# Moving one token subtract a unit from VectorE to GpSimd in the output projection of a two-layer decoder trunk

## The chip, the cores and the metric

The kernel runs on one core of a Trainium2 chip, as one program. The metric is the time of the whole program in device microseconds, and lower is better. Five engines work side by side and meet through semaphores: TensorE (PE; matrix products), VectorE (DVE), ScalarE (ACT), GpSimd (POOL) and SyncE (SP), which here mostly issues DMAs.

## The reference, cut to what matters

The reference is one inference step of a trunk of two layers (one recurrent, one with sliding-window attention) over 2048 prompt tokens and 8 samples, with D = 1024. Each layer ends alike, and the change concerns that end in the second layer:

```python
z = jnp.concatenate([y * jax.nn.silu(g_main), om * jax.nn.silu(g_mem)], axis=-1)   # T x 1536
x = x + z @ w_out[l]                                                               # 1536 x 1024
...
return rmsnorm(x, final_g), ...
```

All is float32. The kernel gets that precision from three passes of a coarser format: each operand is split into a high part (a copy that rounds) and a rest (the value minus the high part), and high times high, high times rest and rest times high are added up.

## The kernel before

Most of the kernel is what comes ahead of this stage: projections, attention and recurrence, up to about 1760 us. The stage of the change is the function `paired`, the last 280 us. It multiplies pairs of token tiles (256 rows) by w_out with Strassen's scheme in Winograd's form: seven products instead of eight. It has 16 units: units 0 to 7 are the eight pairs of token tiles with the first half of the 12 ranks of z, units 8 to 15 the same pairs with the second half, in reverse order. Units 0 and 1 are partly woven into the attention loop ahead; units 1 (its last three products) to 15 follow in `tensor`.

In each unit:

- SyncE loads four blocks of z (`load_z`) into `z_raw`, and the pair's rows of x (`load_x`) after it has stored those of the unit two before. In units 8 to 15 the finished rows are normed and stored as y (`store_y`); the next x goes into their place.
- GpSimd makes four sums of token blocks in place (`sums_tokens`; L2422, L2424, L2426, L2429; 128x384 each): S1, S3, S2, S4. Together with three blocks as loaded (A11, A12, A22) these are the seven token operands, in slots 0 to 6 of `z_raw`: A11, A12, A22, S2, S1, S3, S4.
- ScalarE copies slots 0 to 2 (L2453) and, when GpSimd's fourth sum is done, slots 3 to 6 (L2456) to `z_hi`, the high parts (`tokens_act`).
- VectorE makes the rests `z_lo`, in place over `z_raw`, by three subtracts (`tokens_low`, L2550): slots 0 to 2 (128x1152), slots 3 and 4 (128x768), slots 5 and 6 (128x768).
- TensorE runs seven products (`product`, L2686) in the order P2, P1, P4, P6, P5, P7, P3, each of nine matmuls 128x512 (three thirds k, three passes each). P7 uses slot 5 (S3), P3 slot 6 (S4). P2, P6 and P7 wait for the first, second and third subtract. From the third product on, each waits for the add of two products before.
- VectorE adds each product from its bank to x (`add`, L2566).

The order on each engine is that of its program, and nothing else. VectorE's loop has, for unit u: add P2, P1, P4, P6, then add P5, rest 0 of unit u+1, add P7, rest 1 of unit u+1, add P3, rest 2 of unit u+1. In units 9 and up the norms of the rows finished before stand behind the first or second adds (L2606, L2609). In units 3 to 7 ScalarE also makes the high parts of the weights for units 8 and up, and VectorE their rests (L2543); unit 8 has what is left. One weight block, P3, has its rests made by GpSimd: three subtracts of 128x512 (L2437) between the sums of unit 9 and those of unit 10, and P3 of unit 8 waits for them, a third at a time (`wlop`).

ScalarE's program around there is: keys' DMAs, high parts of P7's weights, first copy of unit 9, high parts of P3's weights, a table load with a square root (L2514), second copy of unit 9 (L2456). Around units 9 to 13 the attention of the 8 samples is woven in (functions named `sm`): TensorE turns sample rows (L1526), GpSimd clears two tiles behind that (L1511, L1512), VectorE works on small tiles (L1653 to L1664), and TensorE takes scores (L1545).

Of the kernel before, what the change touches and what calls it, by code (L numbers as in the profile page):

```python
# [5 lines left out]
F32 = mybir.dt.float32  # L6
F32R = mybir.dt.float32r
ALU = mybir.AluOpType
# [2212 lines left out]
def paired(nc, m, A, outs, it, sm, prior, sums):  # L2221
# [6 lines left out]
    whi, wlo, zhi, zlo, mmd, xn, ss, yn = (signals[n] for n in "whi wlo zhi zlo mmd xn ss yn".split())  # L2228
    sums_z, wlop = prior["tr"], prior["used"]
# [3 lines left out]
    W0, Z0, MM0, XN0, SS0, YN0 = NI, TT, 2 * TP, 2 * TP, 2 * TP, TP  # L2233
    SZ0, WP0 = TP, 4
    LD0, WL0, ONE0 = 16 * (TT // 2), 32, 16

    UNITS, NPROD, KQ = 16, 7, 3
# [5 lines left out]
    P2, P1, P4, P6, P5, P7, P3 = range(NPROD)  # L2243
# [10 lines left out]
    z_raw, z_lo = ([m.at(P + f"z{n}{p}", [128, NPROD, KQ, 128], z_at[p], dt) for p in range(2)] for n, dt in (("raw", F32), ("lo", F32R)))  # L2254
    z_hi = [m.at(P + f"zhi{p}", [128, NPROD, KQ, 128], z_at[p] + NPROD * zq, F32R) for p in range(2)]
# [5 lines left out]
    x_s = m.at(P + "x_s", [128, D], LO + 48 * KB)  # L2261
    w_again = m.at(P + "w_again", [128, NI, D], LO)

    bank = lambda u, i: m.bank[2 * (u % 2) + i % 2]
    sample_bank = m.bank[4]
    phase = lambda u: u // 8
# [145 lines left out]

    def sums_tokens(g, u):
        z, n = z_raw[u % 2], SZ0 + 4 * u
        a21 = z[:, S2, :, :]
        tt = nc.gpsimd.tensor_tensor
        free = lambda i: g.wait_ge(mmd, MM0 + made(u - 2, i)) if u >= 2 else None
        g.wait_ge(*z_loaded(u))  # L2420
        free(P5)
        tt(z[:, S1, :, :], a21, z[:, A22, :, :], ALU.add).then_inc(sums_z, 1)  # L2422
        free(P7)
        tt(z[:, S3, :, :], z[:, A11, :, :], a21, ALU.subtract).then_inc(sums_z, 1)  # L2424
        g.wait_ge(sums_z, n + 2)
        tt(a21, z[:, S1, :, :], z[:, A11, :, :], ALU.subtract).then_inc(sums_z, 1)  # L2426
        free(P3)
        g.wait_ge(sums_z, n + 3)
        tt(z[:, S4, :, :], z[:, A12, :, :], a21, ALU.subtract).then_inc(sums_z, 1)  # L2429

    def pool(g):
        for u in range(UNITS):
            sums_tokens(g, u)
            if u == 9:
                for k in range(KQ):
                    g.wait_ge(whi, W0 + KQ * P3 + k + 2)
                    nc.gpsimd.tensor_tensor(w_lo[1][P3][:, k, :], w_raw[1][P3][:, k, :], w_hi[1][P3][:, k, :].bitcast(F32), ALU.subtract).then_inc(wlop, 1)  # L2437
                sm["pool"](g)
# [10 lines left out]
    def tokens_act(act, u, n):  # L2449
        p = u % 2  # L2450
        if n == 0:
            act.wait_ge(*z_loaded(u))
            nc.scalar.activation(z_hi[p][:, 0:3, :, :], z_raw[p][:, 0:3, :, :], ACT.Copy).then_inc(zhi, 1)  # L2453
        else:
            act.wait_ge(sums_z, SZ0 + 4 * u + 4)
            nc.scalar.activation(z_hi[p][:, 3:7, :, :], z_raw[p][:, 3:7, :, :], ACT.Copy).then_inc(zhi, 1)  # L2456

    def within_act(act, q):
# [81 lines left out]
    def weights_low(v, i, ks=range(KQ)):  # L2540
        for k in ks:
            v.wait_ge(whi, W0 + KQ * i + k + 2)
            nc.vector.tensor_tensor(w_lo[1][i][:, k, :], w_raw[1][i][:, k, :], w_hi[1][i][:, k, :].bitcast(F32), ALU.subtract).then_inc(wlo, 1)  # L2543

    def tokens_low(v, u, n):
        p, e = u % 2, (slice(0, 3), slice(3, 5), slice(5, 7))[n]
        v.wait_ge(zhi, Z0 + 2 * u + min(n, 1) + 1)
        if n == 0:
            v.wait_ge(sums_z, SZ0 + 4 * u + 4)
        nc.vector.tensor_tensor(z_lo[p][:, e, :, :], z_raw[p][:, e, :, :], z_hi[p][:, e, :, :].bitcast(F32), ALU.subtract).then_inc(zlo, 1)  # L2550

    def add(v, u, i):
        extra = 2 if u == UNITS - 1 else 0
        if i == 0:
            v.wait_ge(*loaded_x(u))
            if u in (8, 9):
                v.wait_ge(xn, XN0 + made(u - 1 if u == 8 else u - 3, P3))
        if i in needs:
            v.wait_ge(xn, XN0 + extra + made(u, needs[i]))
        v.wait_ge(mmd, MM0 + (1 if u == UNITS - 1 else 0) + made(u, i))  # L2560
        if i == P7:
            x, y = xt[slot(u)][1][:, :].rearrange("p (n e) -> p n e", n=2), bank(u, i).unsqueeze(1).broadcast_to([128, 2, 512])
        else:
            h, o = part_of[i]
            x, y = xt[slot(u)][h][:, o:o + 512], bank(u, i)
        nc.vector.tensor_tensor(x, x, y, ALU.add).then_inc(xn, 1)  # L2566
# [36 lines left out]
    def norm(v, c, u, h):  # L2603
        n, x = 2 * (u - 8) + 1 - h, xt[slot(u)][h]
        v.wait_ge(ss, SS0 + 2 * n + 2)
        c.link(nc.vector.reciprocal(st[:, 4 + h:5 + h], st[:, 2 + h:3 + h]))  # L2606
        if (u, h) == (8, 0):
            v.wait_ge(fgl, FG0 + 16)
        nc.vector.scalar_tensor_tensor(x[:, :], x[:, :], st[:, 4 + h:5 + h], fg[:, :], ALU.mult, ALU.mult).then_inc(yn, 1)  # L2609

    def add_samples(v, c):
        v.wait_ge(x_ld[2], XS0 + 16)
        v.wait_ge(mmd, MM0 + NPROD * (UNITS - 1) + 1)
        for h in range(2):
            x = x_s[0:NS, 512 * h:512 * h + 512]
            c.link(nc.vector.tensor_tensor(x, x, sample_bank[32 * h + 64:32 * h + 64 + NS, :], ALU.add))
            nc.vector.tensor_tensor(x, x, sample_bank[32 * h:32 * h + NS, :], ALU.add).then_inc(xn, 1)

    def norm_samples(v, c):
        v.wait_ge(ss, SS0 + 2 * (TT - 2) + 2)  # L2620
        c.link(nc.vector.reciprocal(st[0:NS, 8:9], st[0:NS, 7:8]))
        nc.vector.scalar_tensor_tensor(x_s[0:NS, :], x_s[0:NS, :], st[0:NS, 8:9], fg[0:NS, :], ALU.mult, ALU.mult).then_inc(yn, 1)
# [3 lines left out]
    def vector(v, c):  # L2626
        for u in range(1, UNITS):
            for i in range(NPROD):
                if u > 1 or i >= P5:
                    if u == UNITS - 1 and i == 0:  # L2630
                        add_samples(v, c)
                    add(v, u, i)
                if u >= 9 and i in norm_at(u):
                    norm(v, c, u - 1, norm_at(u).index(i))
                if 4 <= u < 8 and i in (0, 2, 3):
                    weights_low(v, u - 4, ((0, 2, 3).index(i),))
                if u == 8 and i < 4:
                    weights_low(v, (P5, P7)[i // 2], ((0, 1), (2,))[i % 2])
                if (u, i) == (9, 2):
                    sm["sum_rows"](v, c)  # L2640
                step = {(9, 6): 0, (10, 5): 1, (11, 3): 2, (12, 1): 3, (13, 0): 4, (13, 4): 5}.get((u, i))
                if step is not None:
                    sm["dve"](v, c, step)
                if (u, i) == (UNITS - 1, P6):
                    norm_samples(v, c)
                if (u, i) == (UNITS - 1, P5):
                    v.wait_ge(ss, SS0 + 2 * (TT - 1) + 1)
                    c.link(nc.vector.tensor_scalar(st[:, 11:12], st[:, 9:10], 1.0 / D, EPS, ALU.mult, ALU.add))
                if u < UNITS - 1 and i >= 4:
                    tokens_low(v, u + 1, i - 4)  # L2650
        last_rows(v, c)

# [12 lines left out]
    def product(pe, u, i):  # L2665
        f, p = phase(u), u % 2
        extra = 2 if u == UNITS - 1 else 0
        if u == 0 and i < 2:
            pe.wait_ge(*after(("b_free", "g_free")[i], NCH * NW + 1))
        if u == 1 and i == 0:  # L2670
            pe.wait_ge(*after("m_ready", it["G"] + it["NQ"]))
        if i in (P2, P6, P7):
            pe.wait_ge(zlo, Z0 + 3 * u + (P2, P6, P7).index(i) + 1)
        if i >= 2:
            pe.wait_ge(xn, XN0 + extra + made(u, i - 2))
        a, al = (z[p][:, of_z[i], :, :] for z in (z_hi, z_lo))
        b, bl = w_hi[f][i], w_lo[f][i]
        for k in range(KQ):
            if u == 0 and k == 0:
                pe.wait_ge(*loaded[0][i])  # L2680
            if (u, i, k) == (0, P3, KQ - 1):
                pe.wait_ge(wlo, W0 + 1)
            if u == 8:
                pe.wait_ge(*((wlop, WP0 + k + 1) if i == P3 else (wlo, W0 + KQ * i + k + 2)))
            for q, (s_, r_) in enumerate(((a, b), (a, bl), (al, b))):
                last = nc.tensor.matmul(bank(u, i), s_[:, k, :], r_[:, k, :], start=(i not in (P6, P7, P3) and k == 0 and q == 0), stop=(k == KQ - 1 and q == 2), skip_group_check=True)  # L2686
        last.then_inc(mmd, 1)
# [399 lines left out]
```

## Time and profile before

| | |
|---|---|
| three runs | 2050.04, 2052.72, 2054.45 us; median 2052.72 |
| profiled execution | 2047.37 us, span 2045.5 us |
| mean granted clock of TensorE | 0.997 |
| busy: TensorE, VectorE, ScalarE, GpSimd | 99%, 64%, 46%, 13% of the span |
| busy in TensorE's L2686 (this stage) | 134.5, 132.5 and 132.2 us in its three passes |

The span is the time from the first to the last instruction of the profiled execution. Busy shares are averages over the whole kernel. The time of an instruction is from its start to its end in the record; where an engine is held while an instruction runs, the record is longer. A matmul of 128x512 is recorded with 0.39 us, but the next starts 0.23 us after it.

### The profile page before, as it was taken

How to read it: one execution, taken by the hardware profiler on the slowest of the kernel's cores; microseconds unless marked ns; L12 is line 12 of the kernel's file. 1: busy time of each engine (PE TensorE's matmuls, PEld its weight loads, DVE VectorE, ACT ScalarE, POOL GpSimd, SP SyncE). 2: the span in 40 equal slices, each digit the busy share in tenths (PEclk: the TensorE clock that was granted, in tenths of full speed). 3: DMA queues.
4: the chain of work that ended last, by engine and by line, in shares of the span. 5: the costliest groups of instructions: out<-in, count | busy, mean ns of one | idle time of the engine just before them, and what ended most of it. 6: DMA issues, size and time to landing. Idle time of an engine off the chain costs nothing.

```text
span 2045.5 us, 34917 instructions
## 1 busy us (share of the span) xinstructions
PE 2020.1 (99%) x14353; PEld 1600.6 (78%) x14353; DVE 1309.9 (64%) x2148; ACT 951.0 (46%) x2061; POOL 274.3 (13%) x249
## 2 busy tenths in 40 slices
PE   9999999999999999999999999999999999999988
PEld 8788887777777777777888888787787778788766
DVE  5845437888888753222634434588888888978766
ACT  6733335778778843212533333444444444422442
POOL 0000002221111100000010000212123330134321
PEclk9999999999999999999999999999999999999999
DMA  9421213442332674354211101222221223777675
GB/s 386 146 65 42 65 39 115 140 137 95 117 107 91 220 257 171 109 191 149 95 58 39 45 20 38 70 86 72 77 78 51 86 71 121 273 248 237 228 276 203
DMA packets 140928, 261.54 MB, mean 128 GB/s; under 512 B 14981, under 2 KB 78501, under 8 KB 136281
## 3 DMA queue, kind: packets, MB, share of 16 engines
q1 hardware_dynamic: 135552, 244.63, 35.0%
q10 hardware_dynamic: 5216, 14.69, 2.0%
q8 instruction: 113, 1.85, 0.4%
q14 instruction: 47, 0.38, 0.1%
HBM read 187.79 MB, written 71.55 MB: 127 GB/s over the span
## 4 chain that ended last, share of the span: by engine, by line
PE 90%; DMA 3%; DVE 3%; ACT 2%; issue 1%; SPq 1%; POOL 0%; ACTq 0%; DVEq 0%; POOLq 0%
PE bank L608 52%; PE bank L2111 12%; PE bank L2686 8%; PE bank L150 2%; PE bank L1174 2%; PE bank L712 2%; PE bank L1160 2%; PE bank L699 2%; DMA in_rows<-in_x_prompt 2%; PE bank L908 1%; PE bank L448 1%; PE bank L628 1%; PE bank L702 1%; DVE wo_lo L1805 0%; DMA op_x<-x_scratch 0%
## 5 line engine op out<-in xcount | busy, mean ns | idle before, releaser
L608 PE MATMUL bank<-x_hi,w_hi 128*128 128x512 f32 x1600 | 636.0, 398 | 0.4 <-DVE w_lo L594 0.4
L608 PE MATMUL bank<-x_hi,w_lo 128*128 128x512 f32 x1600 | 624.1, 390 | 0.0
L608 PE MATMUL bank<-x_lo,w_hi 128*128 128x512 f32 x1600 | 623.2, 389 | 0.0
L608 PEld LDWEIGHTS bank<-x_hi,w_hi 128*128 128x128 f32 x1600 | 300.1, 188 | 96.7 <-issue 35.4
L608 PEld LDWEIGHTS bank<-x_hi,w_lo 128*128 128x128 f32 x1600 | 300.3, 188 | 64.5
L608 PEld LDWEIGHTS bank<-x_lo,w_hi 128*128 128x128 f32 x1600 | 300.5, 188 | 60.8 <-issue 0.7
L2111 PE MATMUL bank<-wo_hi,z_hi 128*128 128x512 f32 x384 | 152.3, 397 | 2.9 <-DVE z_lo L1834 1.2
L2111 PE MATMUL bank<-wo_lo,z_hi 128*128 128x512 f32 x384 | 149.7, 390 | 0.0
L2111 PE MATMUL bank<-wo_hi,z_lo 128*128 128x512 f32 x384 | 149.5, 389 | 0.0
L2686 PE MATMUL bank<-op_whi_p,op_zhi 128*128 128x512 f32 x336 | 134.5, 400 | 10.9 <-DVE op_x L2566 8.4
L758 DVE TENSOR_TENSOR it_P_lo<-bank,it_P_hi 128x512 fp32r<-128x512 f32 x64 | 41.2, 686 | 161.6 <-ACT it_P_hi L753 161.6
L1212 ACT ACTIVATE it_X<-it_X,stat 128x128 f32<-128x128 f32 x256 | 99.2, 389 | 91.4 <-DVE stat L1281 91.4
L653 ACT ACTIVATE it_gh<-bank 128x512 f32<-128x512 f32 x96 | 56.7, 591 | 174.3 <-PE bank L608 172.9
L1338 POOL TENSOR_SCALAR w_raw<-w_raw,prm 128x256 f32<-128x256 f32 x56 | 59.8, 1067 | 545.9 <-PE bank L628 275.1
L2686 PE MATMUL bank<-op_whi_p,op_zlo 128*128 128x512 f32 x336 | 132.5, 394 | 0.0
L2686 PE MATMUL bank<-op_wlo_p,op_zhi 128*128 128x512 f32 x336 | 132.2, 393 | 0.0
L2566 DVE TENSOR_TENSOR op_x<-op_x,bank 128x512 f32<-128x512 f32 (+1 forms) x112 | 85.0, 759 | 61.8 <-PE bank L2686 53.2
L1248 DVE TENSOR_TENSOR it_PTs<-bank,tmask 128x512 f32<-128x512 f32 x128 | 79.5, 684 | 59.3 <-PE bank L150 59.3
L747 ACT ACTIVATE it_Pm<-bank,stat 128x256 f32<-128x256 f32 x128 | 58.9, 472 | 88.2 <-DVE stat L766 88.2
L2111 PEld LDWEIGHTS bank<-wo_hi,z_hi 128*128 128x128 f32 x384 | 72.0, 188 | 24.8 <-issue 3.8
L2686 PEld LDWEIGHTS bank<-op_whi_p,op_zhi 128*128 128x128 f32 x336 | 63.8, 190 | 27.8 <-DVE op_x L2566 10.0
L586 ACT ACTIVATE w_hi<-w_raw,prm 128x256 fp32r<-128x256 f32 x200 | 85.1, 507 | 0.3 <-PE bank L702 0.3
(367 smaller groups left out, 3263.1 us busy)
## 6 DMA issues: line engine op xcount, KB each, us to landing
w_raw<-in_w_items SPq DMA_DIRECT2D x25, 1024.0 KB, 5.1
z_scratch<-it_gz SPq DMA_DIRECT2D x96, 256.0 KB, 2.5
it_cs<-in_rope SPq DMA_DIRECT2D x32, 512.0 KB, 4.1
op_x<-x_scratch SPq DMA_DIRECT2D x28, 512.0 KB, 5.4
z_raw<-z_scratch SPq DMA_DIRECT2D x16, 768.0 KB, 5.0
op_zraw<-z_scratch SPq DMA_DIRECT2D x64, 192.0 KB, 3.4
in_rows<-in_x_prompt SPq DMA_DIRECT2D x4, 2048.0 KB, 27.0
in_x<-in_x_T SPq DMA_DIRECT2D x4, 2048.0 KB, 28.0
```

What stands on the lines that cost most here:

```text
L150: last = nc.tensor.transpose(banks[a][:, 64 * i:64 * i + 64], of(i)[e, :], ident[e, e])
L586: nc.scalar.activation(m.w_hi[w % 2][:, k, :], m.w_raw[w % 2][:, k, :], ACT.Copy, scale=m.prm[:, k, gain(w):gain(w) + 1]).then_inc(S["w_hi ...
L608: last = nc.tensor.matmul(ps, s_, r_, start=(k == 0 and q == 0), stop=(k == KT - 1 and q == 2))
L653: nc.scalar.activation(gh[:, :], PG, ACT.Copy, scale=0.5)
L747: nc.scalar.activation(Pm[:, t, :], (S0, S1)[t // 2][:, (t % 2) * M:(t % 2 + 1) * M], ACT.Exp, bias=negm[:, t:t + 1], scale=MEM_SCALE, acc ...
L758: nc.vector.tensor_tensor(query_half(P_lo, b), (T0, T1)[b].rearrange("p (m t k) -> p m t k", m=2, t=4), query_half(P_hi, b).bitcast(F32), ...
L1212: e = nc.scalar.activation(X[:, j, :], X[:, j, :], ACT.Exp, bias=negm[:, j:j + 1], accum_out=rs[:, j:j + 1])
L1248: r = nc.vector.tensor_tensor(PTs[:, h, a, :].rearrange("p (t b k) -> p t b k", t=4, b=2), by_halves(m.psum, 6, h), m.tmask[:, a, :].rearr ...
L1338: nc.gpsimd.tensor_scalar(raw, raw, m.prm[:, k, gain(w):gain(w) + 1], None, ALU.mult).then_inc(S["zeros"], 1)
L2111: last = nc.tensor.matmul(bank(t, h), s_, r_, start=(first and q == 0), stop=(end and q == 2))
L2566: nc.vector.tensor_tensor(x, x, y, ALU.add).then_inc(xn, 1)
L2686: last = nc.tensor.matmul(bank(u, i), s_[:, k, :], r_[:, k, :], start=(i not in (P6, P7, P3) and k == 0 and q == 0), stop=(k == KQ - 1 and ...
```

## The change

From unit 2 on, the third subtract (slots 5 and 6, the rests of S3 and S4) is GpSimd's and no longer VectorE's. GpSimd does it behind the four sums of the same unit, when ScalarE's second copy of that unit is done, and ahead of whatever its program has next (the sums of the next unit; in unit 9 the three subtracts L2437). It counts on the semaphore of the sums, so their counts move (`sums_at`), as do those of VectorE's rests (`lows_at`). P7 of units 2 and up waits for GpSimd's semaphore. Units 0 and 1 stay as they are. The arithmetic is the same.

```diff
+    sums_at = lambda u: 4 * u if u < 2 else 5 * u - 2
+    lows_at = lambda u: 3 * u if u < 2 else 2 * u + 2
...
+    def tokens_low_pool(g, u):
+        p = u % 2
+        g.wait_ge(zhi, Z0 + 2 * u + 2)
+        nc.gpsimd.tensor_tensor(z_lo[p][:, 5:7, :, :], z_raw[p][:, 5:7, :, :], z_hi[p][:, 5:7, :, :].bitcast(F32), ALU.subtract).then_inc(sums_z, 1)
+
     def sums_tokens(g, u):
-        z, n = z_raw[u % 2], SZ0 + 4 * u
+        z, n = z_raw[u % 2], SZ0 + sums_at(u)
...
     def pool(g):
         for u in range(UNITS):
             sums_tokens(g, u)
+            if u >= 2:
+                tokens_low_pool(g, u)
             if u == 9:
                 for k in range(KQ):
                     g.wait_ge(whi, W0 + KQ * P3 + k + 2)
...
-            act.wait_ge(sums_z, SZ0 + 4 * u + 4)
+            act.wait_ge(sums_z, SZ0 + sums_at(u) + 4)
...
-            v.wait_ge(sums_z, SZ0 + 4 * u + 4)
+            v.wait_ge(sums_z, SZ0 + sums_at(u) + 4)
...
-                if u < UNITS - 1 and i >= 4:
+                if u < UNITS - 1 and 4 <= i < 6:
                     tokens_low(v, u + 1, i - 4)
...
         if i in (P2, P6, P7):
-            pe.wait_ge(zlo, Z0 + 3 * u + (P2, P6, P7).index(i) + 1)
+            if i == P7 and u >= 2:
+                pe.wait_ge(sums_z, SZ0 + sums_at(u) + 5)
+            else:
+                pe.wait_ge(zlo, Z0 + lows_at(u) + (P2, P6, P7).index(i) + 1)
```

## Rows read from the trace of the kernel before

**Rows 1.** The page's first part: busy us, share, instructions.

```profile
PE 2020.1 (99%) x14353; PEld 1600.6 (78%) x14353; DVE 1309.9 (64%) x2148; ACT 951.0 (46%) x2061; POOL 274.3 (13%) x249
```

**Rows 2.** Whom TensorE waited for, 1795 us to the end: total, times, longest.

```profile
PE bank L2686 <- DVE op_x L2566: 7.0, 2, 6.8
PE bank L2686 <- DVE op_zlo L2550: 1.6, 1, 1.6
PE bank L2686 <- issue: 0.6, 1, 0.6
PE bank L1526 <- DVE sm_rows L1520: 0.5, 1, 0.5
```

**Rows 3.** Timeline of TensorE, units 8 to 12: start, duration, [idle before, releaser].

```profile
1898.95 0.47 PE L2686 MATMUL bank<-op_whi_p,op_zhi 128*128 128x512 f32 x1 [0.63 <-issue]
...
1901.10 0.39 PE L2686 MATMUL bank<-op_whi_p,op_zhi 128*128 128x512 f32 x1
...
1903.14 0.40 PE L2686 MATMUL bank<-op_whi_p,op_zhi 128*128 128x512 f32 x1
...
1920.30 0.50 PE L2686 MATMUL bank<-op_whi_p,op_zhi 128*128 128x512 f32 x1 [1.64 <-DVE op_zlo L2550]
...
1924.72 1.92 PE L1545 MATMUL bank<-sm_qs,sm_kw 64*128 64x8 f32 x16
1926.87 0.50 PE L2686 MATMUL bank<-op_whi_p,op_zhi 128*128 128x512 f32 x1 [0.22 <-DVE op_x L2566]
...
1970.97 0.79 PE L2686 MATMUL bank<-op_whi_p,op_zhi 128*128 128x512 f32 x1 [6.80 <-DVE op_x L2566]
...
1974.98 0.54 PE L2686 MATMUL bank<-op_whi_p,op_zhi 128*128 128x512 f32 x1
```

**Rows 4.** Single lines, whole span: durations ns min/median/max, first and last start.

```profile
L2550 DVE TENSOR_TENSOR op_zlo<-op_zraw,op_zhi x48: 945/1194/2147, 1761.0 to 2019.5; 128x768 fp32r<-128x768 f32 x32, 128x1152 fp32r<-128x1152 f32 x16
...
L1341 POOL TENSOR_TENSOR w_lo<-w_raw,w_hi x56: 727/740/1296, 1305.0 to 1685.0; 128x256 fp32r<-128x256 f32 x56
...
L2429 POOL TENSOR_TENSOR op_zraw<-op_zraw x16: 992/1444/2009, 1752.0 to 2007.8; 128x384 f32<-128x384 f32 x16
...
L2437 POOL TENSOR_TENSOR op_wlo_p<-op_wraw_p,op_whi_p x3: 1296/1726/1739, 1894.7 to 1897.7; 128x512 fp32r<-128x512 f32 x3
```

**Rows 5.** Timeline of GpSimd, VectorE and ScalarE in unit 2.

```profile
1816.11 1.01 POOL L2426 TENSOR_TENSOR op_zraw<-op_zraw 128x384 f32<-128x384 f32 x1
1816.21 1.73 DVE L2550 TENSOR_TENSOR op_zlo<-op_zraw,op_zhi 128x768 fp32r<-128x768 f32 x1
...
1817.27 1.55 POOL L2429 TENSOR_TENSOR op_zraw<-op_zraw 128x384 f32<-128x384 f32 x1
...
1818.85 1.50 ACT L2456 ACTIVATE op_zhi<-op_zraw 128x1536 fp32r<-128x1536 f32 x1 [4.80 <-POOL op_zraw L2429]
```

**Rows 6.** Timeline of GpSimd, VectorE and ScalarE in unit 8.

```profile
1894.71 4.69 POOL L2437 TENSOR_TENSOR op_wlo_p<-op_wraw_p,op_whi_p 128x512 fp32r<-128x512 f32 x3 [4.47 <-ACT op_whi_p L2447]
...
1894.82 3.44 DVE L2543 TENSOR_TENSOR op_wlo_p<-op_wraw_p,op_whi_p 128x512 fp32r<-128x512 f32 x2
...
1897.19 1.47 ACT L2456 ACTIVATE op_zhi<-op_zraw 128x1536 fp32r<-128x1536 f32 x1
...
1900.46 1.34 DVE L2550 TENSOR_TENSOR op_zlo<-op_zraw,op_zhi 128x1152 fp32r<-128x1152 f32 x1
```

**Rows 7.** Timeline of ScalarE, VectorE and GpSimd ahead of unit 10.

```profile
1918.10 1.49 ACT L2456 ACTIVATE op_zhi<-op_zraw 128x1536 fp32r<-128x1536 f32 x1 [9.13 <-POOL op_zraw L2429]
...
1918.17 2.08 DVE L2550 TENSOR_TENSOR op_zlo<-op_zraw,op_zhi 128x1152 fp32r<-128x1152 f32 x1 [2.86 <-POOL op_zraw L2429]
...
1918.99 2.13 POOL L2424 TENSOR_TENSOR op_zraw<-op_zraw 128x384 f32<-128x384 f32 x1
```

**Rows 8.** Timeline of ScalarE and VectorE in unit 11.

```profile
1950.63 1.47 ACT L2456 ACTIVATE op_zhi<-op_zraw 128x1536 fp32r<-128x1536 f32 x1
...
1952.57 1.28 DVE L2609 SCALAR_TENSOR_TENSOR op_x<-op_x,stat,op_fg 128x1024 f32<-128x1024 f32 x1
```

**Rows 9.** Windows of 4 us: PE, PEld, DVE, ACT, POOL busy, PEclk, DMA share, GB/s.

```profile
1788.00:1792.00 4.00, 2.59 (x25) 2.08 (x24) 3.96 (x7) 1.17 (x1) 1.34 (x2) 1.00 0.86 314
...
1964.00:1968.00 4.00, 0.17 (x1) 0.00 (x0) 0.00 (x0) 1.16 (x1) 1.70 (x2) 1.00 1.05 395
1968.00:1972.00 4.00, 1.03 (x3) 0.84 (x4) 1.70 (x4) 1.48 (x1) 2.23 (x3) 0.56 1.04 413
```

## What the change should do, predicted before it was measured

> **What bounds the kernel now.** First the page: TensorE is busy for 99% of the span, VectorE for 64%, GpSimd for 13% [rows 1]. So the change can only move the time through TensorE's gaps. The second view is who TensorE waited for, in the stretch in which the changed instruction exists. From 1795 us to the end it waited four kinds of time and 9.7 us in all: 7.0 us for VectorE's adds (6.8 us of it in one piece), 1.6 us for a rest, 0.6 us for "issue" and 0.5 us for the sample rows [rows 2]. The third view, TensorE's timeline, says where: unit 8 before its P7 (0.63 us), before unit 10 (1.64 us) and in unit 10 (0.22 us) [rows 3]. With L1526's these are all of the gaps, and units 2 to 7 have none. A product of nine matmuls takes 2.04 us (P3 of unit 8 starts at 1901.10, the next product at 1903.14 [rows 3]), a unit seven of these, 14.3 us. VectorE keeps up with that nearly everywhere, so its 14 removed instructions are covered by TensorE already.
>
> **What is removed.** In units 2 to 15 VectorE loses one subtract of 128x768 a unit, 14 in all. The shortest of these takes 0.95 us [rows 4], 13.2 us together. On the path that sets the end they are worth only what the gaps give back. Where TensorE has no gap behind VectorE, that is nothing: the matmuls cover it.
>
> **What is added.** GpSimd gets 14 subtracts of 128x768. The trace has none of that size; it has 0.73 us for 256 columns, 0.99 for 384 and 1.30 for 512 at best [rows 4], about 2.2 ns a column on 0.17 us. That makes 1.86 us (bounds: 1.3, the 512 row, and 2.6, two 512s). In a usual unit it is hidden: ScalarE's second copy of unit 4 starts at 1818.85 and takes 1.50 us [rows 5], GpSimd could subtract from 1820.4 to 1822.2, the next four sums are about one unit (14 us) behind the last, and P7 that needs the rest runs a unit later. Unhidden it would cost 1.86 us a unit; I count 0 for all units but 9 and 10.
>
> **The port.** When GpSimd and VectorE both work on tensors in SBUF, one waits until the other's instruction ends. VectorE's subtract begins at 1816.21 and takes 1.73 us instead of 0.95, while GpSimd's runs from 1816.11 to 1817.12; GpSimd's next one begins at 1817.27 and takes 1.55 instead of 0.99, and ends 0.9 us after VectorE's [rows 5]. So they take turns by whole instructions, and a longer GpSimd instruction makes a longer wait. The Trainium skill says the same (SBUF — State Buffer, section "SBUF: two separate sides"): the pair of ports is an exclusive lock and not a split of bandwidth. By that rule the sum below would be as it stands; if the two shared the bandwidth, its first term would be up to 0.9 us smaller.
>
> **Unit 9, where the new wait falls.** In GpSimd's program the new subtract of unit 9 stands ahead of the three subtracts L2437, which make the rests of weight block P3 of unit 8. They have to be there when TensorE comes to P3 (1901.10). Before, they began at 1894.71 and took 4.69 us [rows 6], to 1899.40. Now GpSimd must first wait for ScalarE's second copy of unit 9, which starts only at 1897.19 and takes 1.47 us [rows 6], as weights, a table load and a square root stand ahead of it. Step by step: 1898.7 the wait ends; the new subtract, 1.86 us, to 1900.5; VectorE's subtract of 1152 columns (1.34 us alone [rows 6], about 1.27 behind another) has meanwhile queued and goes next, to 1901.8; first L2437 1.29, to 1903.1; VectorE's subtract of 768 columns, 0.87, and two more L2437, 2.5, to 1906.5. TensorE takes 0.68 us for the last third of P3 and comes to unit 9 at 1907.2 instead of 1903.14: **+4.1 us**. If VectorE never got in between it would be 1898.7 + 1.86 + 3.9 + 0.7 = 1905.2, +2.0, and with 1.3 us for the new subtract +1.5; with 2.6 us for it, and VectorE in between, +4.8. The gap of 0.63 us before P7 goes (the two L2543 that took 3.44 us beside L2437 [rows 6] are alone now), but P3 waits for GpSimd, so this gives nothing. Behind the waiting GpSimd stand only L2437 and, later, the sample memsets and the sums of unit 10, which wait for TensorE's own unit 9 and so move with it.
>
> **Unit 10.** All times here relative to before. GpSimd's sums of unit 11 ran beside VectorE's rests; one of them took 2.13 us [rows 7]. VectorE's first rest took 2.08 us [rows 7] instead of 1.34 and released TensorE at 1920.30. Now GpSimd waits for ScalarE's copy (1918.10, 1.49 us) [rows 7] first: the rest takes 1.34, and TensorE starts 0.73 us earlier. But then the 1.86 us subtract and the four sums run on to 1926 or 1927, beside the small VectorE instructions of the samples, which have to be done before L1545 (1924.72 [rows 3]) and before the add that TensorE waited for at 1926.87. Each can be held up to 1 us. From -0.95 us (0.73 and 0.22 gained, no small one held) to +1.5 us (three held, 0.95 saved). I take **+0.7**, nearer to the upper end, as rows 5 show that any two-input instruction is held.
>
> **Unit 12.** TensorE's 6.8 us are the wait for the tokens' load behind a store of y. The store waits for VectorE's norm at 1952.57, 1.28 us; ScalarE's second copy of unit 12 ends at 1950.63 + 1.47 = 1952.1 [rows 8]. The new subtract starts just there and holds the norm to 1953.96, so it ends 1.4 us later. The DMA engines are full then (share 1.05 with TensorE at 0.17 us of 4 [rows 9]), so what is issued later partly finds the queue emptier: 0 to 1.4, I take **+0.5**. With the engines idle it would be 1.4.
>
> **The clock.** Behind the 6.8 us gap the granted clock fell to 0.56 in that slice; with TensorE busy for 2.59 of 4 us it stayed at 1.00 [rows 9]. In unit 8 it would now do one third of P3, 0.7 us, in the 4.2 us from 1901.1 to 1905.3, which is nearer to the emptier slices of rows 9. The product at the half clock (1.2 GHz) started at 1970.97 and the next at 1974.98, 4.01 us instead of 2.04 [rows 3]. Part of that is hidden by the waits for L2437. Bounds 0 and 2.1; I take **+1.5**.
>
> **The sum.** 4.1 + 0.7 + 0.5 + 1.5 = 6.8 us. The profiled execution took 2047.37 us (span 2045.5 and 1.9 around it) and would take 2054.2; the median of the three runs is 5.35 us higher, which gives 2059.5 us (+0.33%).
>
> **The rivals.** (A) The late rest costs less than 4.1 us: TensorE loses 2.0 to 4 us at P3, the clock holds, unit 10 gives back up to 0.95. The sum is +0.5 to +4, 2053.2 to 2056.8. For it: rows 9 show the clock holding through gaps of 1.4 us, and each term has a low end. Against: L2437's order is fixed, and ScalarE's copy at 1898.7 has no slack. (B) Faster: VectorE sets the pace of a unit, and each subtract taken off it shortens a unit by up to 0.95 us; 14 of them give -13.3, 2039.4 us. It decides where VectorE's work in a unit exceeds TensorE's 14.3 us. Against: TensorE waited for VectorE's adds in two places only [rows 2]; just unit 10 is like this. (C) The change does nothing that is seen: GpSimd's subtract hidden in unit 9 too. That would need ScalarE's copy before 1894.7, and it is 4 us later. Its time would be 2052.7. (D) The 6.8 us gap takes up the delay, if the load that ends it doesn't move with TensorE. The result is 2052.7 to 2054. Against: the norm that starts the store follows a product of unit 11.
>
> **How the numbers follow.** Forecast 0.62, A 0.22, D and C together 0.11, B 0.05. Of no change a measurement of this kernel tells about 0.2%, 4.1 us (2048.6 to 2056.8). The forecast's own range: 5.3 without the fall of the clock, 4.1 if unit 10 and unit 12 cost nothing either, and 4.8 + 1.5 + 1.4 + 2.1 = 9.8 with the high ends, so 2056.8 to 2062.5, and up to 2063.5 should a second place lose its clock. A, C and D lie below 2056.8. The range from 2053.7 to 2063.5 leaves out B, C and the low ends of A and D. Slower 0.62, same 0.33, faster 0.05.
>
> **What would show it.** Right: TensorE's gap ahead of P3 of unit 8 of some 2.5 us and shorter ones between its thirds, released by GpSimd L2437; GpSimd's new line at 1898.7 in its first instruction of that stretch, about 1.86 us each; no gaps in units 2 to 7; the gap at 1920.30 down to 0.9; the norm of unit 10 near 2.7 us long; a granted clock below 1.0 soon after P3. Wrong: the three L2437 done by 1903, a clock of 1.00 through unit 9, or a large gap of unit 12 that is shorter by as much as unit 8 grew.

## The result, and the profile after

| | before | changed |
|---|---|---|
| median of 5 runs each | 2052.72 us | 2060.32 us |
| lowest to highest | 2048.15 to 2056.15 | 2057.48 to 2061.18 |
| profiled execution (span) | 2047.37 (2045.5) | 2061.18 (2059.4) |
| mean granted clock | 0.997 | 0.995 |

The changed kernel is slower: ratio 1.0046, 95% interval 1.0033 to 1.0059. Of 2050 us that is 9.4 us, with 6.8 to 12.1 for the interval; the medians are 7.6 us apart. The forecast was +6.8 us, 2059.5 us, with 2053.7 to 2063.5 for the range. Three executions, one of before and two of an experiment below, ran 22% to 92% longer at a mean clock of 0.505 to 0.750, and no median, interval or ratio here counts them.

In the changed kernel the lines have moved: `product` is L2698 (was L2686), VectorE's `add` L2575 (L2566), its rests L2559 (L2550), ScalarE's second copy L2465 (L2456), the norm L2618 (L2609), GpSimd's rests of weights L2446 (L2437). GpSimd's new subtract is L2420.

The first view is again whom TensorE waited for, from 1795 us on (total, times, longest), to be held against [rows 2]:

```profile
PE bank L2698 <- DVE op_x L2575: 13.5, 7, 6.2
PE bank L1545 <- DVE sm_kw L1658: 1.7, 1, 1.7
PE bank L2698 <- DVE op_zlo L2559: 0.9, 1, 0.9
PE bank L1526 <- DVE sm_rows L1520: 0.6, 1, 0.6
PE bank L2698 <- POOL op_wlo_p L2446: 0.5, 1, 0.5
```

It waited 17.2 us in five kinds, before 9.7 us. VectorE lost 14 instructions and TensorE waits more for VectorE, not less, even without the 2.7 us in the first line that are GpSimd's (see below). Two kinds are new: GpSimd's rests of weights, and VectorE's small instruction L1658. The timeline of TensorE says where; these are all of its gaps from 1795 us to the end except the one of L1526 (0.56 us), and answer to [rows 3]:

```profile
1906.08 0.51 PE L2698 MATMUL bank<-op_whi_p,op_zhi 128*128 128x512 f32 x1 [2.70 <-DVE op_x L2575]
...
1907.98 0.80 PE L2698 MATMUL bank<-op_whi_p,op_zhi 128*128 128x512 f32 x1 [0.55 <-POOL op_wlo_p L2446]
...
1928.33 0.50 PE L2698 MATMUL bank<-op_whi_p,op_zhi 128*128 128x512 f32 x1 [0.90 <-DVE op_zlo L2559]
...
1934.41 1.92 PE L1545 MATMUL bank<-sm_qs,sm_kw 64*128 64x8 f32 x16 [1.68 <-DVE sm_kw L1658]
...
1936.50 0.51 PE L2698 MATMUL bank<-op_whi_p,op_zhi 128*128 128x512 f32 x1 [0.17 <-DVE op_x L2575]
...
1965.50 0.47 PE L2698 MATMUL bank<-op_whi_p,op_zhi 128*128 128x512 f32 x1 [0.32 <-DVE op_x L2575]
...
1968.31 0.50 PE L2698 MATMUL bank<-op_whi_p,op_zhi 128*128 128x512 f32 x1 [0.50 <-DVE op_x L2575]
...
1981.11 0.79 PE L2698 MATMUL bank<-op_whi_p,op_zhi 128*128 128x512 f32 x1 [6.19 <-DVE op_x L2575]
...
2020.55 0.50 PE L2698 MATMUL bank<-op_whi_p,op_zhi 128*128 128x512 f32 x1 [2.17 <-DVE op_x L2575]
...
2024.32 0.47 PE L2698 MATMUL bank<-op_whi_p,op_zhi 128*128 128x512 f32 x1 [1.43 <-DVE op_x L2575]
```

Units 2 to 7 still have no gap. The same places of the program in both profiled executions give the loss as a running difference:

| place | before | changed | difference |
|---|---|---|---|
| last gap of unit 1 (1.41 us in both) | 1789.93 | 1793.09 | 3.2 |
| add behind P2 of unit 9 | 1905.51 | 1914.24 | 8.7 |
| sample rows L1526 | 1912.11 | 1920.84 | 8.7 |
| first product of unit 10 | 1920.30 | 1928.33 | 8.0 |
| L1545 | 1924.72 | 1934.41 | 9.7 |
| product behind the add in unit 10 | 1926.87 | 1936.50 | 9.6 |
| product behind the large gap, unit 12 | 1970.97 | 1981.11 | 10.1 |
| end of span | 2045.5 | 2059.4 | 13.9 |

The first 3.2 us lie ahead of everything that the change touches. There TensorE waited 1.5 us more for the first weights' loads and 1.7 us more for rests of the first layer's output, and the other profiled executions below have this place between 1789.85 and 1791.83. So these are no part of the change, and the change's share of this execution is 10.7 us: 5.6 in units 8 and 9, 0.9 in unit 10, 0.5 to unit 12, 3.8 behind it.

How unit 8 came to it, from the timelines of ScalarE, GpSimd and VectorE of the changed kernel (against [rows 6]):

```profile
1900.19 1.47 ACT L2465 ACTIVATE op_zhi<-op_zraw 128x1536 fp32r<-128x1536 f32 x1
...
1901.74 1.84 POOL L2420 TENSOR_TENSOR op_zlo<-op_zraw,op_zhi 128x768 fp32r<-128x768 f32 x1 [8.50 <-ACT op_zhi L2465]
1903.54 2.39 POOL L2446 TENSOR_TENSOR op_wlo_p<-op_wraw_p,op_whi_p 128x512 fp32r<-128x512 f32 x1
...
1901.97 2.82 DVE L2559 TENSOR_TENSOR op_zlo<-op_zraw,op_zhi 128x1152 fp32r<-128x1152 f32 x1
1904.72 1.21 DVE L2575 TENSOR_TENSOR op_x<-op_x,bank 128x1024 f32<-128x1024 f32 x1
1905.85 0.95 DVE L2559 TENSOR_TENSOR op_zlo<-op_zraw,op_zhi 128x768 fp32r<-128x768 f32 x1
```

GpSimd is idle for 8.50 us and starts when ScalarE's copy ends at 1901.7. VectorE's subtract comes 0.2 us later and takes 2.82 us instead of 1.34: held to 1903.54, then alone to 1904.8. Only then does L2446 run, in 2.39 us from its start in the record, to 1905.93, and TensorE's P3 starts at 1906.08. The page's cause for that gap, "DVE op_x", is the semaphore that came last by its estimate. The program makes P3 wait for the add of P5 and for L2446; that add ran from 1901.37 us and took 0.69 us, so what ended the wait is L2446.

The windows of 4 us (columns as in [rows 9]) show the clock behind it:

```profile
1904.00:1908.00 4.00, 1.38 (x4) 0.65 (x4) 2.80 (x3) 1.45 (x3) 4.00 (x3) 0.80 1.03 362
1908.00:1912.00 4.00, 4.00 (x10) 3.02 (x11) 0.69 (x1) 0.26 (x1) 1.16 (x1) 0.50 0.91 345
1912.00:1916.00 4.00, 4.00 (x16) 3.23 (x15) 1.73 (x3) 2.24 (x4) 0.00 (x0) 0.85 0.11 43
```

It is at the half clock, 1.2 GHz, from about 1906.4 to 1913.2. In the slice that is wholly in it, 10 matmuls are at work in 4 us instead of about 19.

### The profile page after: what moved, and what is told of

It is laid out like the page before. It is cut to its first block, busy times and chain, and to the rows that moved or that the text cites. A ratio compares the mean times of both kernels' runs of the same rounds, so it can differ in the third digit from the quotient of the medians.

```text
span 2059.4 us, 34917 instructions
## 1 busy us (share of the span) xinstructions
PE 2023.7 (98%) x14353; PEld 1601.7 (78%) x14353; DVE 1301.8 (63%) x2134; ACT 951.6 (46%) x2061; POOL 298.5 (14%) x263
## 3 DMA queue, kind: packets, MB, share of 16 engines
q8 instruction: 113, 1.85, 0.4%
## 4 chain that ended last, share of the span: by engine, by line
PE 90%; DVE 4%; DMA 3%; ACT 2%; issue 1%; POOL 1%; SPq 0%; ACTq 0%; DVEq 0%; POOLq 0%
PE bank L608 52%; PE bank L2111 12%; PE bank L2698 8%; PE bank L150 2%; PE bank L1174 2%; PE bank L712 2%; PE bank L448 2%; PE bank L1160 2%; PE bank L699 2%; PE bank L908 1%; PE bank L628 1%; DMA op_x<-x_scratch 1%; PE bank L702 1%; DVE in_x L348 1%; DMA out_y_p<-op_x 1%
## 5 line engine op out<-in xcount | busy, mean ns | idle before, releaser
L2698 PE MATMUL bank<-op_whi_p,op_zhi 128*128 128x512 f32 x336 | 135.7, 404 | 16.4 <-DVE op_x L2575 14.9
L2575 DVE TENSOR_TENSOR op_x<-op_x,bank 128x512 f32<-128x512 f32 (+1 forms) x112 | 85.1, 760 | 79.6 <-PE bank L2698 66.3
L2698 PE MATMUL bank<-op_whi_p,op_zlo 128*128 128x512 f32 x336 | 133.6, 397 | 0.0
L2698 PE MATMUL bank<-op_wlo_p,op_zhi 128*128 128x512 f32 x336 | 133.4, 397 | 0.0
L2698 PEld LDWEIGHTS bank<-op_whi_p,op_zhi 128*128 128x128 f32 x336 | 64.4, 192 | 35.4 <-DVE op_x L2575 15.5
```

## The experiments

Ratios are to runs of the kernel before on the same chip. Their medians were 2049.7 us for unit 9 only, unit 9's behind L2437, units 2 to 8 and units 10 to 15; 2050.7 for unit 10 only, units 12 and 14, and the last row of the table; 2049.5 for the other four. So the medians of two rows can be compared only after their own median of before is taken off. To give GpSimd the subtract of any set of units, the changed kernel's counts were made general:

```diff
+    ON_POOL = tuple(range(2, 16))
-    sums_at = lambda u: 4 * u if u < 2 else 5 * u - 2
-    lows_at = lambda u: 3 * u if u < 2 else 2 * u + 2
+    sums_at = lambda u: 4 * u + sum(w < u for w in ON_POOL)
+    lows_at = lambda u: 3 * u - sum(w < u for w in ON_POOL)
...
-            if u >= 2:
+            if u in ON_POOL:
                 tokens_low_pool(g, u)
...
-                if u < UNITS - 1 and 4 <= i < 6:
+                if u < UNITS - 1 and (4 <= i < 6 or i == 6 and u + 1 not in ON_POOL):
...
-            if i == P7 and u >= 2:
+            if i == P7 and u in ON_POOL:
```

| what | ratio to before | 95% interval | median us |
|---|---|---|---|
| the change (units 2 to 15) | 1.0046 | 1.0033 to 1.0059 | 2060.3 |
| unit 9 only | 1.0030 | 1.0020 to 1.0040 | 2055.8 |
| all, unit 9's behind L2437 | 1.0021 | 1.0013 to 1.0030 | 2054.4 |
| units 2 to 8 only | 1.0000 | 0.9991 to 1.0009 | 2049.6 |
| units 10 to 15 only | 1.0019 | 1.0009 to 1.0029 | 2055.3 |
| nobody makes it | 1.0001 | 0.9989 to 1.0013 | 2050.5 |
| units 10, 11, 13, 15 only | 1.0015 | 1.0005 to 1.0024 | 2052.0 |
| unit 10 only | 1.0008 | 0.9998 to 1.0019 | 2052.8 |
| units 12 and 14 only | 1.0005 | 0.9994 to 1.0016 | 2051.9 |
| none; values early | 0.9971 | 0.9960 to 0.9983 | 2044.0 |
| units 2 to 8; values early, sums wait | 0.9964 | 0.9949 to 0.9978 | 2040.6 |
| none; values early, sums wait | 0.9954 | 0.9938 to 0.9971 | 2040.9 |

### Unit 9 only

```diff
+    ON_POOL = (9,)
```

> Only the subtract of unit 9 is GpSimd's, the 13 others stay VectorE's. If the new wait ahead of L2437 and the clock that falls behind it make most of the loss: +5 to +6 us on before (about 1.0028), TensorE's gaps at P3 of unit 8 as in the changed kernel (2.7 and 0.5 us), granted clock near 0.5 behind them, later gaps as before the change. If instead every moved subtract costs its part of the 9.4 us by the port (14 equal parts): +0.7 us, not to be told from before.

Measured 1.0030 (4.1 to 8.2 us by the interval), two thirds of the loss from one of 14 instructions. TensorE's timeline of this kernel (`product` is L2699, the rests of weights L2447):

```profile
1904.48 0.47 PE L2699 MATMUL bank<-op_whi_p,op_zhi 128*128 128x512 f32 x1 [2.60 <-DVE op_x L2576]
...
1906.38 0.80 PE L2699 MATMUL bank<-op_whi_p,op_zhi 128*128 128x512 f32 x1 [0.97 <-POOL op_wlo_p L2447]
```

and its windows:

```profile
1904.00:1908.00 4.00, 2.55 (x7) 1.71 (x8) 1.21 (x2) 1.45 (x3) 3.56 (x3) 0.78 1.03 390
1908.00:1912.00 4.00, 4.00 (x16) 3.20 (x15) 0.96 (x2) 1.82 (x4) 0.00 (x0) 0.80 0.57 221
```

The same two gaps and the same fall of the clock, shorter here than in the changed kernel; the gaps behind are those of before (1.62, 0.23 and 6.90 us). Equal parts of the port for every moved subtract would have given 0.7 us, which lies outside the interval.

### The change, with unit 9's subtract behind L2437

```diff
-            if u in ON_POOL:
+            if u in ON_POOL and u != 9:
                 tokens_low_pool(g, u)
             if u == 9:
                 for k in range(KQ):
...
+                tokens_low_pool(g, 9)
                 sm["pool"](g)
```

> The change in full, but in unit 9 GpSimd makes its subtract behind the three L2437. If the order in unit 9 is the cause: the gaps of 2.7 and 0.5 us at P3 of unit 8 go, the clock stays at 1.00 there, and the loss falls by 5.7 us, to about +1.5 to +5 us on before, what units 10, 12 and 14 cost. If the port costs it everywhere: still +8 to +9 us.

Measured 1.0021, 0.0025 less than the change, 5.1 us, where 5.7 was expected. TensorE has no gap at P3 of unit 8 any more; GpSimd's timeline shows the rests of weights at the old place and the subtract behind them:

```profile
1896.21 5.14 POOL L2447 TENSOR_TENSOR op_wlo_p<-op_wraw_p,op_whi_p 128x512 fp32r<-128x512 f32 x3 [4.64 <-ACT op_whi_p L2458]
1901.31 2.98 POOL L2421 TENSOR_TENSOR op_zlo<-op_zraw,op_zhi 128x768 fp32r<-128x768 f32 x1
```

The subtract itself takes 2.98 us there, being held, and nobody waits for it. The one gap of TensorE in units 8 and 9 that grew is that of L1526, 1.25 us where the kernel before had 0.55. Together with the run above this shows that the order, and not the work, makes the loss of unit 9.

### Units 2 to 8 only

```diff
+    ON_POOL = tuple(range(2, 9))
```

> GpSimd has the subtracts of units 2 to 8 only. If they are hidden, as no gap of TensorE lies there, 1.000 within 0.1% in either direction, and no gap between 1795 and 1890 us. If VectorE's relief is worth something, up to 7 x 0.95 = 6.6 us faster; if the port costs it, 7 x 0.7 = 4.7 us slower.

Measured 1.0000 within 0.0009: hidden, and worth nothing that can be measured. TensorE has no gap from 1795 to 1890 us. GpSimd's line (durations ns min/median/max) shows that the subtract is never held there:

```profile
L2421 POOL TENSOR_TENSOR op_zlo<-op_zraw,op_zhi x7: 1835/1852/1856, 1796.2 to 1877.4; 128x768 fp32r<-128x768 f32 x7
```

One line of this run's timeline matters for later, a gap in unit 14, in a kernel that differs from before in units 2 to 8 alone:

```profile
2008.78 0.50 PE L2699 MATMUL bank<-op_whi_p,op_zhi 128*128 128x512 f32 x1 [2.91 <-DVE op_x L2576]
```

### Units 10 to 15 only, and its parts

```diff
+    ON_POOL = tuple(range(10, 16))
```

> GpSimd has the subtracts of units 10 to 15 only. By the traces: unit 10 +0.9 us (L1654 and L1655 held to about 1.1 us each, less 0.7 from the earlier first rest), unit 12 +0.8 us (norm held to 2.9 us), unit 14 up to +4.1 us (norm held to 2.1 us, then a load of x that is late): together +1.7 to +5.8 us. If the loss was all unit 9: 0. If unit 14's gap in the profile was chance: +1.7 us and no gap of TensorE behind a load in unit 14.

Measured 1.0019, 3.9 us, inside the expected 1.7 to 5.8. The gaps in unit 11 are there (0.31 and 0.49 us), and unit 14 has two, of 1.08 and 0.80 us: smaller than in the changed kernel, but not gone. With unit 9's 1.0030 and the 1.0000 of units 2 to 8 the parts add up to 1.0049, against 1.0046 for the whole. Three more runs split it: units 10, 11, 13 and 15; unit 10 alone (`ON_POOL = (10,)`); units 12 and 14 alone (`ON_POOL = (12, 14)`).

```diff
+    ON_POOL = (10, 11, 13, 15)
```

> GpSimd has the subtracts of units 10, 11, 13 and 15 only; those of 12 and 14, which held the norms ahead of the late loads of x, are VectorE's again. If the held norm is the cause in units 12 and 14: norms of 1.28 us at these places, no gaps of 0.3 and 0.5 us behind them, and of the loss of units 10 to 15 (1.0019, 3.9 us) what units 10 and 11 cost is left, about +1 us. If the loss in unit 14 is the DMA engines' alone: still up to 4 us, with a gap of 1 to 3 us before a product of unit 14.

Measured 1.0015, 3.1 us: more than the +1 us expected, so by the middle values the norms of units 12 and 14 are not the larger part; the intervals are too wide to show it. They did take 1.28 or 1.29 us, and the gaps of 0.3 and 0.5 us went, as expected. Unit 14 has no gap.

> GpSimd has the subtract of unit 10 only. If the small instructions held behind it (L1654 and L1655 at 1.1 us) and the longer stretch at a low clock behind the gap before L1545 are the cost: the gaps before unit 10 and L1545 are 0.9 and 1.7 us, clock below 1.0 for 6 to 10 us behind, +1 to +3 us (1.0010). If unit 10 only trades 0.7 against 0.9 us as in the prediction: +0.2 us to +0.7 us, ratio within 0.03% of 1.

Measured 1.0008, interval -0.0002 to +0.0019: 1.6 us, in the first expectation's range, but the interval holds the second's too, so the time doesn't tell them apart. The profile has what the first one said, a gap of 1.67 us before L1545 and the clock behind it; windows of unit 10 of this run, to be held against the next three lines, which are those of the kernel before:

```profile
1924.00:1928.00 4.00, 2.33 (x14) 1.72 (x12) 3.90 (x8) 2.91 (x5) 3.78 (x4) 1.00 0.01 0
1928.00:1932.00 4.00, 4.00 (x19) 3.49 (x19) 3.93 (x15) 3.95 (x6) 0.17 (x1) 0.60 0.09 35
1932.00:1936.00 4.00, 4.00 (x16) 3.16 (x14) 1.54 (x2) 0.91 (x1) 0.00 (x0) 0.50 0.82 292
1936.00:1940.00 4.00, 4.00 (x13) 3.43 (x14) 0.00 (x0) 0.00 (x0) 0.00 (x0) 0.50 0.25 87
```

```profile
1924.00:1928.00 4.00, 3.76 (x24) 3.04 (x23) 3.26 (x16) 3.94 (x8) 0.00 (x0) 0.94 0.02 4
1928.00:1932.00 4.00, 4.00 (x19) 2.96 (x17) 3.48 (x5) 3.13 (x3) 0.00 (x0) 0.64 0.38 155
1932.00:1936.00 4.00, 4.00 (x39) 2.90 (x42) 0.69 (x1) 0.00 (x0) 0.00 (x0) 1.00 0.83 259
```

The kernel before is back at 1.00 from 1932 on; the run with unit 10 is at the half clock until past 1942. How long the low clock lasts differs from one profiled execution to the next. An estimate of what it takes is the share of the clock that each window misses, times its 4 us, added up over unit 10 (one profile each):

| profiled execution | missed in unit 10 |
|---|---|
| before; the change; unit 9 only; values early | 1.7 us |
| units 2 to 8; nobody makes it; both with values early and sums waiting | 0 |
| all, unit 9's behind L2437; units 10 to 15; units 10, 11, 13, 15 | 3.4 us |
| units 12 and 14 only, where unit 10 is as before | 3.4 us |
| unit 10 only | 6.8 us |

Every kernel with unit 10's subtract on GpSimd has the gap of 1.66 to 1.68 us before L1545 and lost clock behind it, but so did some without. That the move makes this loss larger is suggested by these rows and not shown. The prediction had no term for it, only 1 us at the top of its range for "a second place". This profiled execution is also the slowest of its 11 runs (2055.12 us), 2.4 us above their median.

> GpSimd has the subtracts of units 12 and 14 only. If the held norm is the cost: norms of 2.9 and 2.1 us there, the gaps of 0.3 and 0.5 us in unit 11, +0.8 us in unit 12 and up to +2 us in unit 14, together +0.8 to +3 us. If the loads of x there are late by the DMA engines alone: 0, ratio within 0.05% of 1.

Measured 1.0005, interval -0.0006 to +0.0016: not told from nothing, nor from the expected 0.8 us. The norms were held, to 2.53 and 2.06 us; one of the two gaps in unit 11 is there (0.48 us), and one of 1.21 us in unit 14.

### Nobody makes the third rest

```diff
+        if u in ON_POOL and i in (P7, P3):
+            al = a
```

GpSimd's new subtract and its counts are taken out again, and P7 waits for ScalarE's copy.

> Nobody makes the third rest of units 2 and up: P7 and P3 of those units take the high part in its place in their third pass, and P7 waits for ScalarE's copy. Same matmuls, 14 subtracts less on VectorE and none more on GpSimd, so this is what the removal alone can give. If VectorE is covered by TensorE: 0.6 us at the gap before P7 of unit 8 and 0.2 us to 1 us at unit 10, together 0 to -2 us, within 0.1% of before. If VectorE set the pace of a unit: -13.3 us.

Measured 1.0001, interval -0.0011 to +0.0013: taking the 14 subtracts away altogether gives nothing that can be measured, and at most 2.3 us by the interval. The gap before unit 10 stayed at 1.65 us and the one of 0.22 us went; one of 1.35 us stood ahead of the large one, which was 5.80 us, and one of 2.63 us in unit 14.

### Where TensorE's large gap comes from

In this run the kernel before has one thing moved, the 4 MB of the samples' values:

```diff
             if u == 11:
-                sm["sp_values"](act)
                 sm["act"](act, 2)
...
+            if u == 10:
+                sm["sp_values"](s)
             if u in (3, 4, 5):
```

> The kernel before with one thing moved: the 4 MB of values for the samples are loaded by SyncE in unit 10, when the scores are done (about 1938 us, DMA share 0.02), and not by ScalarE in unit 11. If the gap of 6.8 us in unit 12 is a full DMA queue: it shrinks to below 2 us and the fall of the clock behind it goes, -6 to -9 us (0.996). If it is the length of the chain norm, store, load itself, whatever else is on the wire: the gap stays at 5 us or more and the time within 0.1%.

Measured 0.9971, 5.9 us faster (3.5 to 8.2 by the interval), just short of the 6 to 9 expected. The large gap in unit 12 is 1.25 us instead of 6.80 and the clock behind it stays at 1.00:

```profile
1966.98 0.50 PE L2687 MATMUL bank<-op_whi_p,op_zhi 128*128 128x512 f32 x1 [1.25 <-DVE op_x L2567]
...
2005.01 0.51 PE L2687 MATMUL bank<-op_whi_p,op_zhi 128*128 128x512 f32 x1 [2.45 <-DVE op_x L2567]
```

In this run the two stores of y in the chain took 3.1 us at the median and the two loads of x behind them 6.9, where before the same four had 7.6 and 8.9. The values' loads were issued from 1940.05 us on here and from 1949.38 before (11 us earlier, as this run was 1.6 us behind at 1790). So most of the 6.8 us was the values' traffic beside the chain, and not the chain's own length. The loads also moved from ScalarE's queue to SyncE's, and no run separates the time of issue from the queue. Some 2.5 us came back in unit 14.

Last, the same with GpSimd's sums of unit 11 held back until VectorE's third rest of unit 10 is done, once with the subtracts of units 2 to 8 on GpSimd and once without:

```diff
+            if u == 11:
+                g.wait_ge(zlo, Z0 + lows_at(10) + 3)
             sums_tokens(g, u)
```

> The useful part of the change with the early values: GpSimd has the subtracts of units 2 to 8 only, the values are loaded in unit 10, and GpSimd's sums of unit 11 wait for the third rest of unit 10, so that they hold neither VectorE's rests nor its small instructions there. If the port is the cause of the 1.6 us gap before unit 10: that gap goes to 0.9 us and the 0.2 us one behind it to 0. Time: 1 to 3 us below the run with the early values alone. If it brings nothing, equal to that run.

> The kernel before with the early values and the wait of GpSimd's sums of unit 11 for the third rest of unit 10, and no subtract on GpSimd at all. If the seven moved subtracts of units 2 to 8 bring nothing, the time is that of the run that has them (0.9964), within 0.1%. If they bring something, 0.1% or more above it.

Measured 0.9964 and 0.9954; their intervals overlap widely, so the seven moved subtracts bring nothing that is seen here either. In both the gap before unit 10 is 0.93 or 0.94 us and the one of 0.22 us behind it is gone, as expected if GpSimd's sums held VectorE there; in both the clock is at 1.00 throughout unit 10. Here are the windows of the first:

```profile
1924.00:1928.00 4.00, 4.00 (x26) 3.37 (x25) 2.35 (x12) 3.63 (x6) 2.08 (x3) 1.00 0.02 4
1928.00:1932.00 4.00, 4.00 (x26) 3.33 (x25) 3.43 (x6) 2.62 (x5) 2.70 (x2) 1.00 0.30 121
```

Against its own median of before each, they are 8.8 and 9.9 us faster, and the run with the early values alone 5.5. But the intervals of the ratios overlap: that the wait adds something to the early values isn't settled by the time. These two are the fastest kernels of the study.

## Why the prediction was right, point by point

**What bounds the kernel.** Right: 14 subtracts less on VectorE are worth nothing that can be measured (1.0001 within 0.0012), and where TensorE has no gap the move costs nothing (1.0000 within 0.0009 for units 2 to 8). Rival B, VectorE as the pace of a unit, and rival C, hidden in unit 9 too, fall with that and with unit 9's run.

**The size of the new instruction.** Forecast 1.86 us from three other sizes, measured 1.85 us at the median of 14 in the changed kernel.

**Unit 9.** The mechanism held: 4.1 us for the late rests of P3 and 1.5 us for the clock, 5.6 together, and 5.6 us in the running difference. By the time, unit 9 alone costs 0.0030, 6.1 us, and putting the subtract behind L2437 gives back 5.1 us. The turns came in the order written: ScalarE's copy, GpSimd's subtract, VectorE's 1152 columns, the first L2446, VectorE's 768. The exact sum is in part luck. The third L2446 ended at 1909.16 us:

```profile
1905.89 3.27 POOL L2446 TENSOR_TENSOR op_wlo_p<-op_wraw_p,op_whi_p 128x512 fp32r<-128x512 f32 x2
```

With 0.1 us to the matmul and 0.68 us for the last third at the full clock, TensorE would have come to unit 9 at 1909.9, which is 3.6 us late when the 3.2 us from before the change are taken off. That leaves 1.9 us for the clock. By this estimate the wait was 0.5 us smaller than forecast and the clock 0.4 larger, still within its bound of 2.1.

**The port in unit 10.** The mechanism was right (L1654, L1655 and L1659 took 1.12, 1.07 and 1.06 us instead of 0.26, 0.29 and 0.25, and the gap before the unit fell from 1.64 to 0.90), and +0.7 stands against +0.9 in the profile of the changed kernel. Its timelines of VectorE and GpSimd, and behind them VectorE's in the kernel before:

```profile
1931.87 1.12 DVE L1654 TENSOR_SCALAR sm_q<-sm_qr,sm_cs 128x72 f32<-128x72 f32 x1
1933.02 1.07 DVE L1655 SCALAR_TENSOR_TENSOR sm_qs<-sm_q,sm_cs,sm_q 128x72 f32<-128x72 f32 x1
1934.13 0.17 DVE L1658 COPY sm_kw<-sm_qs 128x8 f32<-128x8 f32 x1
1934.21 1.06 DVE L1659 SCALAR_TENSOR_TENSOR sm_gz<-sm_gth_s,sm_gh_s 128x96 f32<-128x96 f32 x1
...
1931.91 1.02 POOL L2431 TENSOR_TENSOR op_zraw<-op_zraw 128x384 f32<-128x384 f32 x1
1933.01 0.99 POOL L2433 TENSOR_TENSOR op_zraw<-op_zraw 128x384 f32<-128x384 f32 x1
1934.15 1.01 POOL L2436 TENSOR_TENSOR op_zraw<-op_zraw 128x384 f32<-128x384 f32 x1
```

```profile
1923.82 0.26 DVE L1654 TENSOR_SCALAR sm_q<-sm_qr,sm_cs 128x72 f32<-128x72 f32 x1
1924.12 0.29 DVE L1655 SCALAR_TENSOR_TENSOR sm_qs<-sm_q,sm_cs,sm_q 128x72 f32<-128x72 f32 x1
...
1924.53 0.25 DVE L1659 SCALAR_TENSOR_TENSOR sm_gz<-sm_gth_s,sm_gh_s 128x96 f32<-128x96 f32 x1
```

The size left out the clock behind the new gap. The changed kernel's profile missed as much of it in unit 10 as that of before (1.7 us each), so that the agreement there is partly luck. Units 10, 11, 13 and 15 cost 3.1 us (1.0 to 4.9 by the interval) where the prediction had 0.7 for them: that term was too small. In the profile of that run TensorE is 1.0 us late at L1545, and the clock of unit 10 misses 1.7 us more than before.

**Unit 12.** Forecast +0.5, from a norm held by 1.4 us. The norm was held by 1.6 us, and TensorE came 0.5 us later by the running difference, partly by a new wait for the add that stands behind the norm:

```profile
1961.83 1.85 POOL L2420 TENSOR_TENSOR op_zlo<-op_zraw,op_zhi 128x768 fp32r<-128x768 f32 x1 [5.92 <-ACT op_zhi L2465]
...
1961.88 2.88 DVE L2618 SCALAR_TENSOR_TENSOR op_x<-op_x,stat,op_fg 128x1024 f32<-128x1024 f32 x1
```

GpSimd was there 0.05 us earlier and the norm waited it out. The large gap itself waits for the load of x (in the kernel before, the add there had waited 8.08 us for `op_x<-x_scratch`), not for the tokens' load that the prediction names; the chain norm, store, load is the one it describes. The run with units 12 and 14 alone can't tell this from nothing by its time.

**Unit 14.** Not foreseen: 3.8 us of the changed kernel's profile lie behind unit 12, in gaps of 2.17 and 1.43 us at a late load of x. The prediction had counted 0 there. The change may have a part in it, as the norm ahead of the first was held to 2.06 us and the one ahead of the second to 2.97 us. All four profiles in which GpSimd has the subtracts of units 12 and 14 have gaps in unit 14: 3.6 us together here, 2.5 with unit 9's behind L2437, 1.9 with units 10 to 15, 1.2 with 12 and 14 alone. Of the other six with the values where they were, four have none (before, unit 9 only, unit 10 only, units 10, 11, 13 and 15). But two have it without those subtracts on GpSimd, 2.91 us with units 2 to 8 and 2.63 us with nobody making them. So the late load also comes without the change, and how much of the 3.8 us is the change's stays open.

**The sum.** 6.8 us forecast, 9.4 us by the ratio (7.6 by the medians), 10.7 us in the profile behind the common start. The signs named for being right came: 2.70 us ahead of P3 of unit 8 and a shorter gap inside it, GpSimd's new line at the forecast place once the 3.2 us are taken off (1898.6), 0.90 us before unit 10, a norm of 2.88 us, no gap in units 2 to 7. That the forecast of 2059.5 us lies only 0.8 us from the median is luck: it left out the gaps of unit 14, and its base was a median of three runs that later runs of before undercut by 2 to 3 us. Rival D, that the gap of unit 12 takes up the delay, fell: it went from 6.80 to 6.19 us only, and the norm that starts its chain moved with TensorE (1952.57 before, 1961.88 now). Rival A, less than 4.1 us, is outside the interval.

## What to carry to other kernels

Before an instruction moves to an engine that has time to spare, look at what its program has next, and at which time the thing it will wait for really comes: one wait of 14, ahead of three weight subtracts that TensorE needed, made two thirds of the loss, and three places later the same instruction keeps nobody waiting. Relief for an engine that another covers is worth nothing, here 14 instructions for 0.0001 within 0.0012. Where the profile has a gap, follow its chain to the end: the gap of 6.8 us shrank to 1.25 when a 4 MB load was issued 11 us earlier and by another engine. Just ahead of its old place, from 1940 to 1948 us, the DMA share had been 0.03 and 0.01.

## What the runs showed of the hardware that wasn't expected

A tiny VectorE instruction is held by GpSimd as long as a large one: 128x72 took 1.12 us instead of 0.26 beside sums of 128x384, so many small instructions in a row lose more than one large one: three of them lost 2.5 us together here, the norm of 128x1024 in unit 12 1.6 us. The copy of 128x8 among them (L1658) took 0.17 us as before, but it began at 1934.13, between two of GpSimd's sums (1934.00 to 1934.15), so it doesn't show whether such a copy is held.

The length of TensorE's gap alone doesn't say whether the granted clock falls behind it. It fell behind gaps of 2.60 us (unit 9 only, 0.78 in that slice), 2.67 (no subtract on GpSimd, values early and sums waiting, 0.61) and 2.91 us (units 2 to 8, 0.75). It stayed at 1.00 behind 2.63 us (nobody makes the third rest), 2.45 (values early) and 2.17 us (the changed kernel, unit 14). Behind gaps of only 1.6 to 1.7 us in and before unit 10, with small matmuls around, it fell in nine of the eleven profiles that have such a gap and not in the ones with units 2 to 8 and with nobody making the rest. By the table above that took 0 to 3.4 us among the kernels whose unit 10 is as before, so a gap of this length can cost that much more in one execution than in another.
